# Input stage with eight row buffers, x scaled by diagonal products, and the modulated input made on ScalarE

## The reference, cut to what matters

```python
ada = c @ w_ada[l] + b_ada[l]
shift, scale, gate = jnp.split(ada, 3, axis=-1)
h = rms_norm(x, g_pre[l]) * (1.0 + scale[:, None]) + shift[:, None]
proj = h @ w_in[l]            # 2048 x 11328, float32
...
# rotary angles of q_rope and k_rope from positions; lam from four vectors lambda_*
...
merged = jax.nn.sigmoid(mg_mla) * y_mla + jax.nn.sigmoid(mg_diff) * y_diff
x = x + gate[:, None] * rms_norm(merged @ w_out[l], g_post[l])
```

## Time and profile before

| | |
|---|---|
| median of three, us | 826.92 |
| profiled execution, us | 827.49 |
| its span, us | 825.8 |
| TensorE busy | 774.5 us, 94% |
| VectorE busy | 568.7 us, 69% |
| ScalarE busy | 372.9 us, 45% |
| GpSimd busy | 130.8 us, 16% |
| bytes moved | 190.23 MB, 230 GB/s over the span |

### The profile page before, as it was taken

One profiled execution on the slowest core, in us unless ns is written; L12 is line 12 of the kernel. 1 busy time (PEld: TensorE's weight loads), 2 busy tenths in 40 slices (PEclk: granted clock), 3 DMA queues, 4 the chain that ended last, 5 costly groups with the idle time before them and its releaser, 6 DMA issues.

```text
span 825.8 us, 9913 instructions
## 1 busy us (share of the span) xinstructions
PE 774.5 (94%) x3617; PEld 637.9 (77%) x3617; DVE 568.7 (69%) x835; ACT 372.9 (45%) x529; POOL 130.8 (16%) x147
## 2 busy tenths in 40 slices
PE   3299999999999899999999999989999999999995
PEld 2277888888887788888888777768788888877884
DVE  4589887988864765554556689878867676565544
ACT  4234434334356366444454655455444444434441
POOL 1000000000000000000004263542454444210000
PEclk9589999999999999999999999999999999999998
DMA  7799999999864455555538776567768867775542
GB/s 235 256 344 332 357 337 327 327 324 316 270 192 141 152 158 162 165 153 153 153 102 285 238 243 202 183 200 226 254 213 279 266 224 250 286 250 201 200 156 103
DMA packets 116811, 190.23 MB, mean 230 GB/s; under 512 B 9813, under 2 KB 42778, under 8 KB 116250
## 3 DMA queue, kind: packets, MB, share of 16 engines
q1 hardware_dynamic: 115776, 189.43, 69.8%
q10 hardware_dynamic: 986, 0.17, 0.1%
HBM read 187.47 MB, written 2.10 MB: 230 GB/s over the span
## 4 chain that ended last, share of the span: by engine, by line
PE 80%; DVE 8%; DMA 4%; issue 4%; ACT 3%; POOL 1%; ACTq 1%; SPq 0%; DVEq 0%; POOLq 0%
PE ps L1539 24%; PE ps L1541 24%; PE ps L1540 24%; DVE w_lo L1284 2%; DMA w_raw<-in_w_out 2%; PE ps L1328 2%; ACT w_hi L846 1%; DVE ada_acc L1080 1%; DMA lam_in<-in_lambda_k 1%; PE ps L1373 1%; PE ps L1412 1%; PE ps L1382 1%; PE ps L1386 1%; ACT probs L692 1%; DMA ada_ring<-in_w_ada 1%
## 5 line engine op out<-in xcount | busy, mean ns | idle before, releaser
L1284 DVE TENSOR_TENSOR w_lo<-w_raw,w_hi 128x1024 fp32r<-128x1024 f32 x249 | 305.2, 1232 | 158.9 <-ACT w_hi L846 157.7
L846 ACT CAST w_hi<-w_raw 128x1024 fp32r<-128x1024 f32 x249 | 260.3, 1051 | 325.8 <-PE ps L1541 240.0
L1539 PE MATMUL ps<-w_hi,h_hi 128*128 128x512 f32 x704 | 286.7, 407 | 13.4 <-issue 7.8
L1541 PE MATMUL ps<-w_hi,h_lo 128*128 128x512 f32 x704 | 278.1, 395 | 0.0
L1540 PE MATMUL ps<-w_lo,h_hi 128*128 128x512 f32 x704 | 278.0, 395 | 0.0
L1539 PEld LDWEIGHTS ps<-w_hi,h_hi 128*128 128x128 f32 x704 | 134.4, 191 | 43.2 <-issue 11.4
L1541 PEld LDWEIGHTS ps<-w_hi,h_lo 128*128 128x128 f32 x704 | 134.5, 191 | 29.7
L1540 PEld LDWEIGHTS ps<-w_lo,h_hi 128*128 128x128 f32 x704 | 134.7, 191 | 27.4 <-issue 0.7
L1080 DVE SCALAR_TENSOR_TENSOR ada_acc<-ada_ring,cols,ada_acc 128x512 f32<-128x512 f32 x112 | 78.5, 747 | 1.1 <-DMA ada_ring<-in_w_ada 1.0
L510 POOL TENSOR_SCALAR gate_ring<-gate_ring,cols 128x512 f32<-128x512 f32 x28 | 50.7, 1810 | 62.5 <-DMA gate_ring<-in_w_ada 61.9
L1539 PE MATMUL ps<-w_hi,o_hi 128*128 128x512 f32 x128 | 50.7, 396 | 0.0
(11 more groups left out here) (220 smaller groups left out, 708.4 us busy)
## 6 DMA issues: line engine op xcount, KB each, us to landing
w_raw<-in_w_in SPq DMA_DIRECT2D x177, 512.0 KB, 4.6
ada_ring<-in_w_ada SPq DMA_DIRECT2D x128, 256.0 KB, 5.4
gate_ring<-in_w_ada SPq DMA_DIRECT2D x32, 512.0 KB, 5.0
w_raw<-in_w_out SPq DMA_DIRECT2D x32, 512.0 KB, 3.6
w_raw<-in_w_o_mla SPq DMA_DIRECT2D x16, 512.0 KB, 4.6
w_raw<-in_w_o_diff SPq DMA_DIRECT2D x16, 512.0 KB, 5.8
w_raw<-in_w_ukv SPq DMA_DIRECT2D x8, 512.0 KB, 4.2
x_tok<-in_x SPq DMA_DIRECT2D x2, 1024.0 KB, 6.8
```

Source lines behind the costliest of these rows:

```text
L846: act.copy(w_hi[:, p % RING, :], w_raw[:, p % RING, :]).then_inc(hi_done, 1)
L1284: dve.tensor_tensor(w_lo[:, p % RING, :], w_raw[:, p % RING, :], w_hi[:, p % RING, :].bitcast(F32), ALU.subtract).then_inc(lo_done, 1)
L1539: mm(o, lhsT=s_hi[:, k, q], rhs=hi, start=first and r == 0, stop=False)
L1541: ins = mm(o, lhsT=s_lo[:, k, q], rhs=hi, start=False, stop=last and r == tiles - 1)
```

## The change

1. The ring of row parts has eight slots, four in the old place and four in the space of `r_b` (`ada_slot`). `read_q`, which writes into that space, waits until all 64 parts are used.
2. `angles` moves from the head of VectorE's order to behind piece PH1 - 6, the lambda products to behind PH1 - 3, sine and cosine on ScalarE to behind piece PH1 - 1. Their five loads move from ScalarE's queue to SyncE's, at pieces 40 and 42 to 45; the load of `pos_row` moves from piece 8 to 41.
3. x is transposed by a product with the diagonal of the inverse root, `x_tok` tile times `x_diag`, 32 float32 matmuls in place of 32 transposes, two spreading products and one copy. They start only when `x_diag` is there, which VectorE makes after its third row part, as before.
4. TensorE transposes the accumulators, eight 128x128 transposes into banks 6 and 7 (`turn_ada`). ScalarE sums them with four activations that have an accumulator output, makes `mod_shift` and `mod_gain` with four one-column activations, then `h_hi` with two and the unrounded h with two more (`make_h`). VectorE keeps one subtraction of 512 columns for `h_lo`. 1 + scale bias times gain is formed once at the start.
5. `make_h` and `make_h_lo` of pair j stand two pieces behind the last piece of period j - 1, pair 0 behind piece 0 (`h_after`).
6. Periods 0 and 1 begin with a visit and not with a q step. The parts of group 1 are taken two at a time ahead of pieces 1 to 4; in later periods the first part comes one piece earlier.
7. TensorE waits for `h_hi` before the first piece that uses a pair and for `h_lo` only before the third matmul; a visit that follows a `turn_ada` waits for ScalarE's reading of the sums (`ada_read`), no longer for `mod_ready`.

```diff
 RING = 4
+ADA_RING = 8
...
-    [0, (("vd", 0), (0,)), 1, (("vd", 1), (0,)), 2, (("gate", 0), (0,))],
-    [0, (("gate", 1), (0, 1)), 1, (("gate", 2), (0, 1)), 2],
+    [(("vd", 0), (0,)), 0, (("vd", 1), (0,)), 1, (("gate", 0), (0,)), 2],
+    [(("gate", 1), (0, 1)), 0, (("gate", 2), (0, 1)), 1, 2],
...
-                ada_before.setdefault(own[1 + q * (len(own) - 1) // (KT // 2)], []).append((j + 1, q))
+                place = 1 + q // 2 if j == 0 else q * (len(own) - 1) // (KT // 2)
+                ada_before.setdefault(own[place], []).append((j + 1, q))
...
-        mod_after = {first_part[j][0]: j for j in range(2, KT // 2)}
-        mod_after |= {0: 0, first_part[0][-1]: 1}
-        h_hi_after = {p + 1: j for p, j in mod_after.items() if j >= 2} | {2: 0, first_part[0][-1]: 1}
-        h_lo_after = {p + (j >= 2): j for p, j in mod_after.items()}
+        h_after = {0: 0} | {place + 2: j for place, j in sum_before.items()}
...
+        ada_slot = lambda n: ada_rings[n % ADA_RING // 4][:, n % 4, :, :, :]
...
-                if n >= RING:
-                    sp.wait_ge(ada_used, n - RING + 1)
+                if n >= ADA_RING:
+                    sp.wait_ge(ada_used, n - ADA_RING + 1)
...
+            def make_h(j):
+
+                eng.wait_ge(ada_turned, j + 1)
+                for b in range(4):
+                    ins = act.activation(sum_junk[:, b, :, :], ps[:, 6:8, b * P:(b + 1) * P], ACT.Copy,
+                                         accum_out=mod_sums[:, b:b + 1])
+                ins.then_inc(ada_read, 1)
+                eng.wait_ge(ada_read, j + 1)
+                for k in (2 * j, 2 * j + 1):
+                    act.activation(mod_shift[:, k:k + 1], mod_sums[:, k % 2:k % 2 + 1], ACT.Identity,
+                                   bias=cols[:, V_SHIFT + k:V_SHIFT + k + 1])
+                    ins = act.activation(mod_gain[:, k:k + 1], mod_sums[:, 2 + k % 2:3 + k % 2], ACT.Identity,
+                                         scale=cols[:, V_GPRE + k:V_GPRE + k + 1],
+                                         bias=cols[:, V_SCALE + k:V_SCALE + k + 1])
+                ins.then_inc(mod_ready, 1)
+                eng.wait_ge(mod_ready, j + 1)
+                for k in (2 * j, 2 * j + 1):
+                    ins = act.activation(h_hi[:, k, :], xnT[:, k, :], ACT.Identity, scale=mod_gain[:, k:k + 1],
+                                         bias=mod_shift[:, k:k + 1])
+                ins.then_inc(h_hi_ready, 1)
+                if j >= 1:
+                    eng.wait_ge(h_lo_ready, j)
                 for b in range(2):
                     k = 2 * j + b
...
+                    ins = act.activation(stage[:, 0, b * SEQ:(b + 1) * SEQ], xnT[:, k, :], ACT.Identity,
+                                         scale=mod_gain[:, k:k + 1], bias=mod_shift[:, k:k + 1])
+                ins.then_inc(h_full_ready, 1)
...
             def make_h_lo(j):
...
+                eng.wait_ge(h_full_ready, j + 1)
+                dve.tensor_tensor(h_lo[:, 2 * j:2 * j + 2, :].rearrange("p k s -> p (k s)"), stage[:, 0, :],
+                                  h_hi[:, 2 * j:2 * j + 2, :].rearrange("p k s -> p (k s)").bitcast(F32),
+                                  ALU.subtract).then_inc(h_lo_ready, 1)
...
-            angles()
...
+                if p in h_after:
+                    make_h_lo(h_after[p])
+                if p == PH1 - 6:
+                    angles()
+                if p == PH1 - 3:
+                    mix_products()
...
+            def turn_ada(j):
 
                 pe.wait_ge(ada_used, (j + 1) * (KT // 2))
                 if j:
-                    pe.wait_ge(mod_ready, j)
+                    pe.wait_ge(ada_read, j)
...
+                for t in range(2):
+                    for b in range(4):
+                        ins = tr(ps[:, 6 + t, b * P:(b + 1) * P], acc[:, t, b * P:(b + 1) * P], ident[:, :])
+                ins.then_inc(ada_turned, 1)
...
+                        ins = mm(ps[:, g % 6, b * SEQ + t * P:b * SEQ + (t + 1) * P],
+                                 lhsT=x_tok[:, t, k * P:(k + 1) * P], rhs=x_diag[:, t, :], start=True, stop=True)
                 ins.then_inc(xT_made, 1)
...
                 if p < PH1 and p == first_use[i]:
-                    pe.wait_ge(h_lo_ready, i + 1)
+                    pe.wait_ge(h_hi_ready, i + 1)
...
+                    if p < PH1 and p == first_use[i] and (r, t) == (0, 0):
+                        pe.wait_ge(h_lo_ready, i + 1)
                     ins = mm(o, lhsT=s_lo[:, k, q], rhs=hi, start=False, stop=last and r == tiles - 1)
```

More of the change, by code:

```diff
@@ L296, in hybrid_block @@
         raw_in = [sem(f"raw_in{i}") for i in range(RING)]
-        ada_in = [sem(f"ada_in{i}") for i in range(RING)]
+        ada_in = [sem(f"ada_in{i}") for i in range(ADA_RING)]
         gate_in = [sem(f"gate_in{i}") for i in range(2)]
@@ L447, in _ @@
                 sp.dma_start(dst, piece_source(kind, n, i)).then_inc(raw_in[p % RING], 16)
-                if p == 8:
+                if p == 40:
+                    with nc.allow_non_contiguous_dma(reason="256 positions, once"):
+                        sp.dma_start(pos_q[:, :], positions[0, :].rearrange("(t p) -> p t", p=P)).then_inc(pos_in, 16)
+                if p == 41:
                     sp.dma_start(pos_row[:, :], positions[0, :].partition_broadcast(P)).then_inc(pos_row_in, 16)
+                if 42 <= p < 46:
+                    v = (lambda_q1, lambda_k1, lambda_q2, lambda_k2)[p - 42]
+                    sp.dma_start(lam_in[:, p - 42, :], v[0, :].partition_broadcast(P)).then_inc(lam_ld, 16)
                 for k in gate_parts_at.get(p + 1, ()):
@@ L1191, in make_h @@
-            def make_h(j):
-                eng.wait_ge(mod_ready, j + 1)
-                if j == 0:
-                    eng.wait_ge(root_row_ready, 1)
-                else:
-                    eng.wait_ge(h_lo_ready, j)
-                for b in range(2):
-                    k = 2 * j + b
-                    ins = dve.scalar_tensor_tensor(out=stage[:, 0, b * SEQ:(b + 1) * SEQ], in0=xT[:, k, :],
-                                                   scalar=mod_gain[:, k:k + 1], in1=root_row[:, :], op0=ALU.mult,
-                                                   op1=ALU.mult)
-                ins.then_inc(h_full_ready, 1)
@@ L1205, in make_h_lo @@
-            def make_h_lo(j):
-                eng.wait_ge(h_hi_ready, j + 1)
-                for b in range(2):
-                    k = 2 * j + b
-                    ins = dve.scalar_tensor_tensor(out=h_lo[:, k, :], in0=stage[:, 0, b * SEQ:(b + 1) * SEQ],
-                                                   scalar=mod_shift[:, k:k + 1], in1=h_hi[:, k, :].bitcast(F32),
-                                                   op0=ALU.add, op1=ALU.subtract)
-                ins.then_inc(h_lo_ready, 1)
+            def make_h_lo(j):
+                eng.wait_ge(h_full_ready, j + 1)
+                dve.tensor_tensor(h_lo[:, 2 * j:2 * j + 2, :].rearrange("p k s -> p (k s)"), stage[:, 0, :],
+                                  h_hi[:, 2 * j:2 * j + 2, :].rearrange("p k s -> p (k s)").bitcast(F32),
+                                  ALU.subtract).then_inc(h_lo_ready, 1)
@@ L1325, in ada_sum @@
                 acc = acc_of_group(j)
-                for b in range(4):
-                    for t in range(2):
-                        ins = mm(ps[:, 6, b:b + 1], lhsT=acc[:, t, b * P:(b + 1) * P], rhs=ones[:, 0:1],
-                                 start=t == 0, stop=t == 1)
-                ins.then_inc(ada_summed, 1)
+                for t in range(2):
+                    for b in range(4):
+                        ins = tr(ps[:, 6 + t, b * P:(b + 1) * P], acc[:, t, b * P:(b + 1) * P], ident[:, :])
+                ins.then_inc(ada_turned, 1)
             def group(g):
```

109 lines of the change are left out of this document (43 added, 66 removed).

## The result

Four executions of the changed kernel took 813.74 to 818.53 us, median 816.51; four of the kernel before on the same chip 826.29 to 829.0, median 827.31. The ratio is 0.9865, 95% interval 0.9831 to 0.9899: 10.8 us faster. The forecast was 812.0, with a range of 806 to 821.

What follows compares the result with a forecast made beforehand. TensorE sets the pace; time is saved where it idles, runs slowly or does other than piece matmuls. Gains 5.3 + 5.0 + 2.4 + 3.8 = 16.5 us off 827.5, 1.3 kept back for small stalls: 812 us, range 806 to 821.

Steps and rivals of the forecast that it cites:

- T(1): T(j) is when pair j's turn (before: sums) ends; T(1) was forecast at 53.5 us against 58.78, gain 5.3.
- my 9.6: Start: the 32 diagonal-product matmuls take 5.3 us at half clock plus 4.3 us after it, done at 26.5.
- Period 0: First period: bound by VectorE, whose eight parts and `w_lo` of pieces 1 to 4 take 15.2 us.
- The rival of the clock: Clock stays half through diagonal products (4.2 us) or falls at T(1) and T(2) (1.6 us each): 816.5 us, chance 0.17.
- so the longer ScalarE chain is covered by 0.6 us: Later periods: fourth piece's `w_lo` is ready at T + 7.6, TensorE wants it at T + 8.15.
- Periods 3 to 6: Each takes 28.1 us in place of 29.04, the turn replacing 1.69 us of sums by 0.9; gain 3.8.
- costed at nothing: Moved angles, sine, cosine and six small loads at pieces 40 to 45 fit into slack and cost no time.
- Behind T(7) nothing of TensorE's work changes: After the last turn: TensorE's work stays the same, so gains were summed only up to T(7).
- Transfers: Rival: only 345 GB/s can be held where period 1 asks for 383; costs 3 to 5 us, 816 us, chance 0.12.
- The chain: Rival: unpipelined ScalarE chain to `h_lo` of 6.8 us loses 7.4 us in seven periods, 1.7 at start: 821 us, chance 0.09.
- Table loads: Rival: two table loads of 1.28 us per `make_h` block make it slower than before: 836 us, chance 0.05.
- More than forecast: Rival: VectorE's first parts land earlier without the lambda loads and nothing stalls: 807 us, chance 0.07.

Runs made afterwards that it cites:

- a_first: The changed kernel with VectorE doing the row parts that belong to the next piece before `h_lo`, not behind it: 807.64 us, ratio 0.9763.
- a_late: The changed kernel with its six small loads at pieces 59 to 64 in place of 40 to 45: 815.15 us, ratio 0.9844.
- a_nopool: The changed kernel with GpSimd's three operations on odd gate rows cut to 8 of 512 columns, no version to keep: 809.47 us, ratio 0.9772.
- b_ring8: The kernel before with eight row-part slots and nothing else: 823.66 us, ratio 0.9928.
- a_first_again: a_first run once more, on the chip of a_first_cast0: 807.99 us, ratio 0.9762.
- a_first_cast0: a_first with ScalarE's rounding of piece 0 between the copies of x, not behind the last: 808.43 us, ratio 0.9756.
- b_order1: The kernel before with only the order of period 1 changed, so that it begins with a visit: 825.54 us, ratio 0.9955.
- b_both_h0: The kernel before with ring of eight, moved angles, and `h_hi` of pair 0 behind piece 0 in place of piece 2: 816.36 us, ratio 0.9852.
- a_again: The changed kernel run again unchanged, for a second trace: 815.93 us, ratio 0.9857.

## Why the prediction was right or wrong

**The start was right in its steps.** Forecast and measured: first piece matmul 31.9 and 30.3, T(1) 53.5 and 51.9, T(2) 74.0 and 73.1, T(3) 96.6 and 96.0. The 1.6 us at the beginning are the 326 GB/s of the first 16 us in place of the 249 I carried over from the kernel before: VectorE began its parts at 10.07, TensorE the diagonal products at 14.71 in place of 16.9. Their 10.27 us are 0.7 over my 9.6: 28 records at 0.213 us where I took 25, the rest at 0.11. (The price of that rival was a little off: 13.7 in place of 9.6 is 4.1 us, not 4.2.) Period 0 was bound by VectorE, as forecast; a_first shows it, since two parts taken before `h_lo` and not after it shortened it by 1.8 us. The 1.6 us that came early are luck: I didn't forecast them, they are hardly more than the start moves from trace to trace, and they hide as much of the losses that follow.

**Clock and later periods, 1 and 2.** At T(1) TensorE waits 1.2 us for the copy and then turns for 1.06 us, and no half clock follows; none follows T(2). Period 1 gained 4.3 us (forecast 5.0), period 2 2.2 (2.4). Of the 0.7 us that period 1 took over its forecast (21.2 against 20.5), 0.4 are TensorE's wait for `w_lo` of piece 9: it is 0.9 us where I had 0.5. The rival of the clock, 816.5 us, gives almost the measured time and is false all the same: what it prices did not happen.

**The step that failed** is "so the longer ScalarE chain is covered by 0.6 us". Periods 3 to 6 should have taken 28.1 us each and gained 3.8; they took 28.3, 28.6, 29.8 and 28.6 and gained 0.9. ScalarE's timeline behind T(4), where period 4 begins; T is here 123.97, the start of the first piece matmul behind the turn:

```profile
124.26 0.38 ACT L843 ACTIVATE sum_junk<-ps 128x256 f32<-128x256 f32 x1 [1.09 <-PE ps L1330]
...
125.60 0.22 ACT L843 ACTIVATION_READ_ACCUMULATOR sum_junk<-ps 128x1 f32 x1
125.86 0.30 ACT L848 ACTIVATE mod_shift<-mod_sums,cols 128x1 f32<-128x1 f32 x1
...
126.52 0.37 ACT L850 ACTIVATE mod_gain<-mod_sums,cols 128x1 f32<-128x1 f32 x1
126.93 1.09 ACT L856 ACTIVATE h_hi<-xnT,mod_shift,mod_gain 128x256 fp32r<-128x256 f32 x2
127.93 1.08 ACT L863 ACTIVATE stage<-xnT,mod_shift,mod_gain 128x256 f32<-128x256 f32 x2
```

The distances of the starts are the terms of my sum. The turn's handover to ScalarE takes 0.29 us, which I had left out. The four sums take 1.60 (forecast 2.0), the four one-column activations 1.07 (0.7), `h_hi` 1.00 (0.9), `stage` until VectorE starts 1.11 (0.9), the subtraction 0.69 (0.65). That is 5.76 us from T to the end of `h_lo`, against 5.1. The difference of 0.6 is the whole cover. VectorE then goes on without a gap:

```profile
129.04 0.69 DVE L1209 TENSOR_TENSOR h_lo<-stage,h_hi 128x512 fp32r<-128x512 f32 x1 [2.78 <-ACT stage L863]
129.65 1.41 DVE L1105 SCALAR_TENSOR_TENSOR ada_acc<-ada_ring,cols,ada_acc 128x512 f32<-128x512 f32 x2
130.98 1.22 DVE L1285 TENSOR_TENSOR w_lo<-w_raw,w_hi 128x1024 fp32r<-128x1024 f32 x1
```

`w_lo` of the fourth piece is there at 132.20, T + 8.23, and TensorE wanted it at T + 8.15. So the cover was used up, but at that piece TensorE lost only 0.1 us. The larger loss of periods 4 and 6 stands three pieces later, where my sum didn't look. The seventh piece is the first of the period's second visit, and it may begin only when VectorE has added the first visit's sum out of banks 6 and 7. That addition stands in VectorE's queue behind the late parts:

```profile
139.58 1.13 DVE gate_part_sum L967
```

```profile
140.33 0.39 PE L1541 MATMUL ps<-w_hi,h_lo 128*128 128x512 f32 x1
140.81 0.47 PE L1537 MATMUL ps<-w_hi,h_hi 128*128 128x512 f32 x1
```

The addition ends at 140.71, and the starts are 0.48 us apart in place of 0.23; with the slower matmul behind it the piece costs 0.3 us more. The same stands at 170.6 and 199.3 us. The idle 2.78 us in front of `h_lo` are the remedy that I did not see: a row part of 1.33 us that is ready fits into them. That is a_first, and there both losses are gone. The waits of TensorE for single releasers from 28 to 235 us (us in total, times, longest), the changed kernel and then a_first; of the three for `w_lo`, one of 0.8 us is in period 0, one of 0.9 in period 1 and one of 0.6 in period 5:

```profile
PE ps L1537 <- ACT h_hi L856: 4.5, 1, 4.5
PE ps L1537 <- DVE w_lo L1285: 2.3, 3, 0.9
```

```profile
PE ps L1540 <- ACT h_hi L856: 4.5, 1, 4.5
...
PE ps L1540 <- DVE w_lo L1286: 0.2, 1, 0.2
```

For the one-column activations my value came from a 64-column row without a per-partition operand. The Trainium skill, "ScalarE: Activation LUTs", section "What ACT_TABLE_LOAD costs", gives 186 ns and 0.833 ns per element for an activation, 93 ns more for each per-partition operand, and an overlap of 93 ns back to back. By that the four would take some 1.0 us (an estimate from the page); the trace agrees with 1.07, and its `mod_gain` row of 0.37 us, with two such operands, is the page's 0.37.

**Period 5** lost another 1.2 us to the small loads, which I had costed at nothing. ScalarE stood waiting for piece 42's load when the turn ended at 152.7, so its sums began late, and with them the next visit, which waits for their reading, and `h_lo`; in a_late they didn't. The changed kernel, then a_late:

```profile
153.12 1.05 ACT L871 CAST w_hi<-w_raw 128x1024 fp32r<-128x1024 f32 x1 [2.95 <-DMA w_raw<-in_w_in]
154.08 0.37 ACT L843 ACTIVATE sum_junk<-ps 128x256 f32<-128x256 f32 x1
```

```profile
149.95 1.06 ACT L871 CAST w_hi<-w_raw 128x1024 fp32r<-128x1024 f32 x1 [1.60 <-DMA w_raw<-in_w_in]
151.81 0.39 ACT L843 ACTIVATE sum_junk<-ps 128x256 f32<-128x256 f32 x1 [0.80 <-PE ps L1330]
```

**"Behind T(7) nothing of TensorE's work changes"** held for the work and not for its time. The angles were hidden: 14.2 us of gain at `w_lo` of piece 72. The end of the stage then leaves TensorE idle for some 5 us in either kernel, and the half clock behind it lasted 6.8 us where it had lasted 3.4, which costs about 1 us. The windows of the kernel before and of the kernel after, behind that idle stretch:

```profile
268.00:276.00 8.00, 4.51 (x13) 3.55 (x14) 7.76 (x15) 0.05 (x1) 0.00 (x0) 0.79 0.46 133
```

```profile
256.00:264.00 8.00, 6.67 (x18) 5.24 (x19) 7.80 (x16) 1.05 (x1) 0.00 (x0) 0.57 0.25 67
```

At 451 us TensorE waited 2.01 us for `probs` where it had waited 0.99, since VectorE's part of the gate sum took 1.79 us; a second half clock, of 3.4 us, came right behind. Of the kernel before, and then of the kernel after, VectorE and GpSimd:

```profile
459.06 1.29 POOL L513 TENSOR_TENSOR ada_acc<-ada_acc,gate_ring 128x512 f32<-128x512 f32 x1
...
461.40 0.75 DVE L1080 SCALAR_TENSOR_TENSOR ada_acc<-gate_ring,cols,ada_acc 128x512 f32<-128x512 f32 x1
```

```profile
447.37 2.14 POOL L521 TENSOR_TENSOR ada_acc<-ada_acc,gate_ring 128x512 f32<-128x512 f32 x1
...
448.27 1.79 DVE L1105 SCALAR_TENSOR_TENSOR ada_acc<-gate_ring,cols,ada_acc 128x512 f32<-128x512 f32 x1
```

Before, GpSimd had ended 1.05 us before VectorE began; after, the two overlap, and VectorE's instruction takes 1.04 us more. In a_nopool, at the same place, it takes 0.74 again:

```profile
447.10 0.74 DVE ada_acc L1105
...
450.76 0.55 PE ps L1413 x3
```

TensorE's wait there is 0.98 us, no half clock follows, and the whole stretch behind piece 72 is 6.7 us shorter. That shows the overlap to be the cause at this place. How much it cost there is read from the lead over the kernel before, in us, at the end of `w_lo` of five pieces (451 us lies between pieces 124 and 144):

| `w_lo` of piece | 78 | 124 | 144 | 156 | 248 |
|---|---|---|---|---|---|
| changed kernel | 14.2 | 13.1 | 10.4 | 11.2 | 11.0 |
| a_nopool | 15.0 | 14.3 | 15.8 | 15.9 | 18.9 |

The doubled half clock took 1.0 us and the place at 451 us took 2.7; 0.7 came back. a_nopool loses nothing at 451 us. What it gains beyond that is no loss of the change, since the kernel before does GpSimd's work too: its edit relieves VectorE elsewhere. The Trainium skill, "SBUF — State Buffer", section "Who interferes with whom", says that a VectorE instruction with two SBUF inputs and a GpSimd instruction that reads SBUF contend for a shared port pair, that this pair is an exclusive lock, and that the order of issue decides who is blocked. The trace agrees: VectorE's instruction, which began second, ended 0.55 us after GpSimd's, a little less than its own length.

Why the first half clock doubled stays open. It lasts 3.4 us in the kernel before, b_ring8, a_first, a_first_again and a_first_cast0, and 6.8 us in all the others. The moved angles don't decide it: b_order1 leaves them where they were and has 6.8, a_first moves them and has 3.4.

**The rivals.** Transfers: mostly false. Period 1 took 21.2 us, 0.7 over the forecast, at a mean of 346 GB/s; it did not need 383, since the transfers had run ahead from 10 us on, and a_first did the same period in 20.2. The one late load that told was that of period 5. The chain: true in kind, 1.7 us over periods 3 to 6 (115.3 - 4 x 28.1 = 2.9, less the 1.2 of period 5) in place of 7.4 over seven. Table loads: false, there is none within `make_h`. More than forecast: its early landing came true, its second half did not.

**The sum.** Forecast 16.5 by its steps, minus 1.3 kept back. Measured 6.9 + 4.3 + 2.2 + 0.9 = 14.3 at T(7), minus 3.4 behind it. Of the 5.6 us between 16.5 and 10.9, 3.4 lie behind T(7) and 2.9 in periods 3 to 6, 0.9 in periods 1 and 2, and the early start gives 1.6 back. The largest single miss is the stretch behind T(7), which I had put at nothing. With the start as forecast the time would have been some 818 us, still inside the range.

## What to carry to other kernels

Where an engine waits for a chain and then has to work through a queue, put what is ready ahead of the wait: moving the parts ahead of `h_lo` brought 8 of the 20 us here, 5.8 of them in the stretch that it touches. A cover of 0.6 us under a chain of thirteen instructions is no cover; every handover of 0.1 to 0.3 us has to be in that sum. And a late queue has to be followed to whatever else stands in it: in periods 4 and 6 the addition that frees two banks cost more than the piece for which the sum was made. A stretch whose work is untouched can still lose what was gained ahead of it, because it now runs at another phase against GpSimd; look at its waits in a trace, not only at its length.

The version that beats both kernels is a_first, 807.6 and 808.0 us in two comparisons, ratio 0.976. The ring, the move of the angles and one changed place for `h_hi` (b_both_h0, 0.9852 [0.9818, 0.9887]) give as much as the whole change. Whether parts ahead of `h_lo` would help there too was not tried; its periods 3 to 6 take 29.05 us each, as before, and TensorE never waits for `w_lo` in them, so the move would have little to win there.

## What the runs showed of the hardware

- A float32 multiply-add of 128x512 on VectorE with two inputs in SBUF took 1.79 us beside a GpSimd addition of two SBUF tensors, and 0.75 us alone; a subtraction of 128x1024 took 2.26 us in place of 1.23 in a_again, again beside one of 1.27 us on GpSimd:

```profile
446.80 1.27 POOL L521 TENSOR_TENSOR ada_acc<-ada_acc,gate_ring 128x512 f32<-128x512 f32 x1
...
446.89 2.26 DVE L1285 TENSOR_TENSOR w_lo<-w_raw,w_hi 128x1024 fp32r<-128x1024 f32 x1 [5.59 <-ACT w_hi L871]
```

- With all issues queued the transfers ran at 382 to 401 GB/s in every window of 2 us from 10 to 36 us of the changed kernel, not only in one of 4 us.
- The stretches at half clock in these traces last 3.4 us or 6.8 us, apart from those at start and end; the same idle stretch of 4.7 us was followed by either.
- Neither 1.68 us of one-column sums without a wait (b_order1) nor a wait of 1.19 us with 1.06 us of transposes behind it (the changed kernel) brought the half clock; the same wait with 1.98 us of sums behind it (the kernel before) did.
